# Gate unit of the mLSTM mixer: low halves beside the high halves in one tile, two products in place of three

## What is computed

```python
p = h @ w_in
qk, v, o, gates = jnp.split(p, [2 * A_QK, 2 * A_QK + A_V, 2 * A_QK + 2 * A_V], axis=-1)
...
gates = (gates + b_if).astype(jnp.float32).transpose(0, 2, 1)
log_i = gates[:, :A_HEADS]
log_f = jax.nn.log_sigmoid(gates[:, A_HEADS:])
```

## Time and profile before

| | |
|---|---|
| median of 3 runs | 1891.04 us |
| lowest, highest | 1889.8, 1891.27 us |
| span of the profiled execution | 1888.3 us |
| PE busy | 1858.5 us (98%) |
| DVE busy | 1441.9 us (76%) |
| ACT busy | 879.5 us (47%) |

### The profile page before, as it was taken

The page is one execution under the profiler, slowest core; times in us unless marked ns, Lnnn a source line. Parts: engine busy times, 40 slices in busy tenths (PEclk is TensorE's granted clock), DMA queues, the critical chain, the costliest instruction groups (busy, mean ns, idle before and its releaser), DMA issues.

```text
span 1888.3 us, 30173 instructions
## 1 busy us (share of the span) xinstructions
PE 1858.5 (98%) x11724; PEld 1675.6 (89%) x11724; DVE 1441.9 (76%) x2013; ACT 879.5 (47%) x1398; POOL 55.6 (3%) x40
## 2 busy tenths in 40 slices
PE   7999999999999999999999999999999999999997
PEld 5799998898779999998899999889877799999886
DVE  6978878696677888868788888796788778888434
ACT  6356542244344665642255565224444455656321
POOL 4300000000000100000010000000000010000000
PEclk9999999999999999999999999999999999999999
DMA  9623359634213333259743322972321243322432
GB/s 381 243 102 112 111 189 334 233 90 160 64 56 110 125 112 106 94 186 322 270 133 114 111 91 83 350 255 91 108 71 45 68 135 112 112 99 95 138 97 83
DMA packets 86003, 273.51 MB, mean 145 GB/s; under 512 B 8561, under 2 KB 18929, under 8 KB 84889
## 3 DMA queue, kind: packets, MB, share of 16 engines
q1 hardware_dynamic: 85712, 271.83, 41.7%
q10 hardware_dynamic: 200, 0.52, 0.1%
HBM read 261.82 MB, written 10.50 MB: 144 GB/s over the span
## 4 chain that ended last, share of the span: by engine, by line
PE 93%; DVE 3%; DMA 1%; ACT 1%; issue 1%; SPq 0%; POOL 0%; DVEq 0%; ACTq 0%
PE acc L702 14%; PE acc L704 14%; PE acc L703 14%; PE outp L703 13%; PE outp L704 13%; PE outp L702 13%; PE stats L702 3%; PE stats L704 3%; PE stats L703 3%; DMA raw<-w 1%; PE outp L1001 1%; DVE w_lo L1712 1%; PE acc L1097 1%; PE stats L1124 0%; PE acc L982 0%
## 5 line engine op out<-in xcount | busy, mean ns | idle before, releaser
L702 PE MATMUL acc<-h_hi,w_hi 128*128 128x256 f32 (+1 forms) x1220 | 398.0, 326 | 9.4 <-DVE w_lo L1712 4.7
L703 PE MATMUL acc<-h_lo,w_hi 128*128 128x256 f32 (+1 forms) x1220 | 389.2, 319 | 0.0
L704 PE MATMUL acc<-h_hi,w_lo 128*128 128x256 f32 (+1 forms) x1220 | 389.2, 319 | 0.0
L1213 ACT ACTIVATE w_hi<-arena 128x1024 fp32r<-128x1024 f32 (+2 forms) x231 | 209.8, 909 | 373.4 <-DMA arena<-w 184.9
L1922 DVE TENSOR_TENSOR w_lo<-arena,w_hi 128x1024 fp32r<-128x1024 f32 (+1 forms) x272 | 290.4, 1088 | 107.2 <-ACT w_hi L1290 103.7
L1712 DVE TENSOR_TENSOR w_lo<-arena,w_hi 128x1024 fp32r<-128x1024 f32 (+2 forms) x229 | 239.6, 1049 | 147.2 <-ACT w_hi L1213 145.7
L1290 ACT ACTIVATE w_hi<-arena 128x1024 fp32r<-128x1024 f32 (+1 forms) x272 | 257.7, 949 | 76.1 <-PE stats L704 28.5
L702 PE MATMUL outp<-g_hi,w_hi 128*128 128x512 f32 (+1 forms) x792 | 290.2, 366 | 0.0
L703 PE MATMUL outp<-g_lo,w_hi 128*128 128x512 f32 (+1 forms) x792 | 289.5, 365 | 0.0
L704 PE MATMUL outp<-g_hi,w_lo 128*128 128x512 f32 (+1 forms) x792 | 289.4, 365 | 0.0
L702 PEld LDWEIGHTS acc<-h_hi,w_hi 128*128 128x128 f32 x1220 | 232.5, 191 | 31.7 <-issue 8.9
(11 more groups left out here) (284 smaller groups left out, 3429.5 us busy)
## 6 DMA issues: line engine op xcount, KB each, us to landing
arena<-w SPq DMA_DIRECT2D x174, 512.0 KB, 3.8
ada_raw<-ada SPq DMA_DIRECT2D x64, 512.0 KB, 6.1
arena<-ada SPq DMA_DIRECT2D x56, 512.0 KB, 6.0
arena<-w SPq DMA_DIRECT2D x64, 384.0 KB, 3.4
arena<-w SPq DMA_DIRECT2D x64, 320.0 KB, 4.6
arena<-wa SPq DMA_DIRECT2D x33, 512.0 KB, 3.5
arena<-wb SPq DMA_DIRECT2D x32, 512.0 KB, 3.5
early_ada<-ada SPq DMA_DIRECT2D x8, 1024.0 KB, 17.6
```

Of the source, the lines that this page charges most:

```text
L702: pe.matmul(bank, a_hi, b_hi, start=start, stop=False, skip_group_check=onto)
L703: pe.matmul(bank, a_hi, b_lo, start=False, stop=False, skip_group_check=onto)
L704: return pe.matmul(bank, a_lo, b_hi, start=False, stop=stop, skip_group_check=onto)
L1213: act.activation(w_hi[base % SLOTS][:, 0:n], src[:, 0:n], ACT.Copy).then_inc(hi_ready, 1)
```

## The change

The gate unit uses eight of 128 columns. The changed kernel writes the low halves of these columns into unused columns of the high tile itself: column c goes to column 64 + c. So one tile `both` holds the high halves in the columns 0 to 3 and 32 to 35 and the low halves in 64 to 67 and 96 to 99. PE multiplies it with the high half and with the low half of h, 16 matmuls in place of 24. The products of the low halves come out in the partitions 64 to 67 and 96 to 99 of `aux`, and DVE adds them to the others in its gate chain. The low by low product, which was left out, is now part of the sum.

```diff
             def mixer_a():
                 U, T = U_A, T_A
+
+                def gate_unit():
+
+                    pe.wait_ge(lo_ready, U + 9)
+                    for k in range(KT):
+                        both = block_of((U + 8) % SLOTS, k)[0]
+                        pe.matmul(aux[:, :], both, h_hi[:, k, :], start=k == 0, stop=False)
+                        last = pe.matmul(aux[:, :], both, h_lo[:, k, :], start=False, stop=k == KT - 1)
+                    last.then_inc(unit_done, 1)
+
                 first_group(U, T, 1)
                 for s in range(4, 8):
                     take_acc(T, s)
                     unit(U + s, 0, acc[:, s % 4, :])
-                unit(U + 8, 0, aux[:, :])
+                gate_unit()
                 v_half(U + 9, T, 8)
...
+                def gate_low():
+
+                    dve.wait_ge(hi_ready, U + 9)
+                    both = w_hi[(U + 8) % SLOTS][:, :].rearrange("p (k c) -> p k c", c=P)
+                    src = raw[(U + 8) % RAWS].rearrange("p (k c) -> p k c", c=P)
+                    dve.tensor_tensor(both[:, :, 64:64 + 36], src[:, :, 0:36], both[:, :, 0:36].bitcast(F32),
+                                      ALU.subtract).then_inc(lo_ready, 1)
+
...
-                    low_part(U + t + 4)
+                    if t == 4:
+                        gate_low()
+                    else:
+                        low_part(U + t + 4)
 
                 link(dve.memset(rows_one[:, :], 1.0))
                 dve.wait_ge(unit_done, U + 9)
                 dve.wait_ge(small_loaded, 32)
                 R = [rows[:, n, :] for n in range(8)]
-                dve.tensor_scalar(R[0], aux[0:HEADS, :], gbias[:, 0:1], None, ALU.add).then_inc(dve_step, 1)
-                link(dve.tensor_copy(R[1], aux[32:32 + HEADS, :]))
+                dve.tensor_copy(R[1], aux[32:32 + HEADS, :]).then_inc(dve_step, 1)
+                dve.tensor_copy(R[2], aux[96:96 + HEADS, :]).then_inc(dve_step, 1)
+                dve.tensor_copy(R[0], aux[64:64 + HEADS, :]).then_inc(dve_step, 1)
+                chain[0] += 3
+                dve.wait_ge(dve_step, chain[0])
+                link(dve.scalar_tensor_tensor(out=R[2], in0=R[1], scalar=gbias[:, 1:2], in1=R[2],
+                                              op0=ALU.add, op1=ALU.add))
+                dve.wait_ge(dve_step, chain[0])
+                dve.scalar_tensor_tensor(out=R[0], in0=aux[0:HEADS, :], scalar=gbias[:, 0:1], in1=R[0],
+                                         op0=ALU.add, op1=ALU.add).then_inc(dve_step, 1)
                 chain[0] += 1
-                dve.wait_ge(dve_step, chain[0])
-                link(dve.tensor_scalar(R[2], R[1], gbias[:, 1:2], None, ALU.add))
                 dve.tensor_scalar(R[4], R[2], 0.0, None, ALU.min).then_inc(dve_step, 1)
```

## The result

The changed kernel takes 1893.47 us, median of 20 runs (1891.81 to 1894.57). The kernel before took 1891.13 us beside it (20 runs, 1889.8 to 1891.77). The ratio is 1.0013, with the 95% interval [1.0007, 1.0019]: slower by 2.3 us, inside the 0.2% of the forecast, but more than the 0.8 us that it named. The profiled execution has a span of 1891.9 us against 1888.3. Among all executions of this document two stand far out, one of the kernel before (3770.75 us) and one of the changed kernel with the copies first (6021.9 us); without them no median moves by more than 0.1 us.

The account below looks back on a forecast made before the run. PE, working 98% of the span, was taken as the bound. Its 1.81 us saving becomes a wait, and the gate chain (1.59 longer, 0.77 earlier) adds 0.8: 1891.04 + 0.8 = 1891.8 us, range 1889.0 to 1893.8.

Parts of the forecast that it names:

- PE's gate unit is shorter: mLSTM gate unit on PE: 16 matmuls remain of 24, at 0.227 us each, so PE is done 1.81 us earlier.
- low half of U+8, start to start: DVE ahead of the gate chain: the smaller low half costs 0.36 us instead of 1.13, making DVE 0.77 us earlier.
- memset to the last step ahead of f_arg_ready: DVE's gate chain: added copies and sums lengthen this stretch from 2.94 to 4.53 us, 1.59 us longer.
- issue of U+15 behind m_rows_ready: SP's DMA queue: U+15's load is issued 1.85 us after the gate chain's end, behind the row's store and load.
- The wait that eats the gain: Second half of v: PE comes at 454.75, starts about 457.4, waiting 2.6 us for ACT's copy of bank 0.
- the chain: From m_rows_ready through U+15's load and ACT's copy of bank 0 to PE: fixed length, 8.79 us, not passing through PE.
- the row's trip: SP's queue: the row's store, waiting for m_rows_ready, and its spread load stand ahead of U+15's load.
- Rival 1: Second half of v: the gain arrives, PE starts at 454.75 and the kernel takes 1889.2 us; chance 0.10.
- The shift of the gate chain: End of DVE's gate chain, m_rows_ready: 1.59 us longer less 0.77 earlier, so 0.8 us later (0.44 to 1.33).
- The landing of U+15: DMA ahead of ACT's high half: U+15 lands 5.26 us after its issue, a distance taken as fixed.
- Rival 2: After PE's new 2.6 us gap at v: the clock falls, costing 1.6 us more, 1893.4 us in all; chance 0.12.
- the likeliest case: Whole kernel: a wait eats PE's 1.81 us gain and 0.8 us more is lost, 1891.8 us; chance 0.70.

Follow-up runs that it names:

- changed kernel with the copies first: Changed kernel, but ACT and DVE copy out the four banks of acc ahead of U+15's high and low halves: 1889.74 us, ratio 0.9993.
- the kernel before with the copies first: Kernel before, with ACT and DVE copying out the four banks ahead of U+15's halves, nothing else: 1890.63 us, ratio 0.9998.
- the long chain: Kernel before, with only its gate chain on DVE replaced by that of the changed kernel, adding zeros: 1894.15 us, ratio 1.0013.

## Why the prediction was right, and where it was off

The sum named seven numbers, and the profile after has them all:

| step | forecast | measured |
|---|---|---|
| PE's gate unit is shorter | 1.81 | 1.81 |
| low half of U+8, start to start | 0.36 | 0.36 |
| memset to the last step ahead of f_arg_ready | 4.53 | 4.52 |
| m_rows_ready, from the start of the gate unit | +0.8 | +0.81 |
| issue of U+15 behind m_rows_ready | 1.85 | 1.85 |
| landing of U+15 behind its issue | 5.26 | 5.71 |
| PE's wait at bank 0 | 2.6 | 3.04 |

**The wait that eats the gain: right, and shown.** Taking away either link of the chain (the row's trip, or the order of ACT's list) puts PE 1.6 to 1.8 us ahead of the kernel before, and in the kernel before it moves PE by less than 0.03. Rival 1 is out.

**The shift of the gate chain: right.** The low half and the copies cost what like rows of before said. The copies stand 0.71 and 0.72 us apart, each 0.03 us behind the end of the one ahead. That was the value taken (0.70) and not the 0.60 of overlapping ones. The rule of the Trainium skill, page "VectorE: DVE Perf Modes", section "Two Vector instructions with no wait between them", holds them for their other group of partitions, and the trace agrees.

**The landing of U+15: the term that was mis-sized.** I took the distance from the one value that I had, 5.26 us. The eleven profiles in which this load stands behind the row's load have 5.26 to 5.76 us, and the kernel before had the least of them. It isn't the change that made it longer: the kernel before with the copies first, whose list of loads is the same, has 5.70. The text named this as where the sum fails most easily ("if the distance between the row's store and the landing of U+15 isn't fixed"). It cost 0.45 us. So PE was 0.81 + 0.45 = 1.26 us late at bank 0, not 0.8.

**The clock: the step that failed.** Rival 2 had the right mechanism, place and price (1.6 us), but a chance of 0.12. I set it by "my gap would be 2 us shorter than the only one that did it". The gap that the text set against it, 1.7 us "after which the clock held", was misread: PE ran at half pace there already, as shown above with the long chain. What the trace of before had was a fall after 4.56 us and none after 1.49, and everything between them was open; that says nothing against a fall at 2.6. The profiles: it fell after waits of 3.04, 3.02 and 1.86 us, and held after 1.42 and 1.18 and where the gap was filled. The Trainium skill warns of idle gaps between bursts of matmuls from a certain length on (page "TensorE: Matmul & The Clock Gate", section "Why this matters for your kernels"). That a gap brings the clock down, the runs here agree; but 1.86 us is shorter than the gaps that the page warns of, and there the measurement decides.

**The sum with both.** 1.26 + 1.6 = 2.9 us at the scores, as the table has it (105.68 against 102.83). The profile's span is 3.6 us longer: 0.2 from stages ahead, and 0.6 behind the scores. A part of that 0.6 stands in the first mixer's projection, a stage in which the changed kernel's PE waits 0.24 us:

```profile
597.31 0.70 PE L800 MATMUL stats<-sumsq,ones 128*128 128x256 f32 x2 [0.24 <-DVE sumsq L1823]
```

The medians are 2.3 us apart. Rival 2's time, 1893.4, is the measured 1893.47: what came was that rival and not the likeliest case. The measured time lies inside the stated range because the range, 4.8 us wide, took in both rivals. That rival 2's figure fits to 0.1 us is partly luck: its share of 0.8 us for the wait was 1.26.

One more reading ahead of the sum was wrong, without effect: the largest wait of PE was called 4.7 us, but the list of waits of the kernel before has another of 6.5, at the very start, before any other matmul.

## What to carry to other kernels

Work taken from the engine that is busy 98% of the time is a gain only as far as everything that it meets next was done ahead of its need by as much. Read how many hundredths of a microsecond each releaser was ahead of its need, and follow it back to something that the change doesn't move; here it was a load queued behind a row's round trip, and each of two small moves turned 2.3 us lost into PE standing 1.6 to 1.8 us ahead at the scores (some 1.4 in the medians, which the noise alone could make). A wait of 2 to 3 us on TensorE should be priced with the clock's fall behind it, unless rows of the same length show that it holds.

## What the runs showed of the hardware

- The granted clock fell to 0.50 after a gap of only 1.86 us in one profile and of 3.0 us in two, and each fall cost 1.6 us. It held after 1.42 and 1.18 us at the same place, and after 1.49 near the start.
- Behind the first waits of the program the matmuls run at half pace (0.21 us apart, later 0.11 for the same shape) while the granted clock is printed as 1.00, so the clock there is to be read from the distances.
- The load of one weight unit lands 3.5 to 3.6 us after its issue when it stands ahead of the row's load in the queue (three profiles), and 5.26 to 5.76 us when it stands behind it (eleven).
- Loads of the same size at the same place of the program differ from one profile to the next by about as much as the change was worth: in the second mixer's projection from 3.5 to 5.6 us.
